# Mixed right sides moved behind the last low part, and a last step taken by halves of the tokens, in a two-layer fp32 kernel

## The chip, the cores and the metric

The kernel runs on one core of one Trainium2 chip. The metric is device time in microseconds (us) of one execution, the median of several. TensorE (PE in the rows) multiplies, VectorE (DVE), ScalarE (ACT) and GpSimd (POOL) work elementwise, and SyncE (SP) issues most of the DMAs. "Span" is the time from the first to the last instruction of the profiled execution.

## What is computed

Two transformer blocks, one after the other, on one sequence of 1024 tokens with 1024 features, all in fp32 accuracy:

```python
# first block
h = rmsnorm(x, norm1_g); proj = h @ w_in
... # differential attention (4 heads) and forgetting attention (8 heads)
x = x + mix @ w_out
h2 = rmsnorm(x, norm2_g)
x = x + (silu(h2 @ w_gate) * (h2 @ w_up)) @ w_down
x = rmsnorm(x, normf_g)
# second block
p = rmsnorm(x, g_attn) @ w_in_2
... # two causal convolutions and a stick-breaking attention (8 heads)
x = x + concat([y_a, y_b, y_c]) @ w_out_2
x = x + square(relu(rmsnorm(x, g_ffn) @ w_ff1)) @ w_ff2
out = rmsnorm(x, g_final)
```

## The kernel before

**Layout and precision.** Activations lie transposed: 128 features on the partitions, tokens along the row. A tensor of 1024 features is 8 tiles `e` of 128 x 1024, and a "half" is 512 tokens, the width of one PSUM bank. Every fp32 product is made of three fp32r matmuls: high part of the weights times high part of the right side (L1610), low weights times high right side (L1612), high weights times low right side (L1615). High parts of weights (`wh`) are made by ScalarE (L2176), low parts (`lows`, written over the loaded `values`) by GpSimd (L2414), for pieces of 128 x 512 that SyncE loads. The first matmul of a piece waits for its high part, the second for its low part; the third waits for the low part of the right side.

**The border between attention and feed-forward**, once per block (near 640 and near 1790 us). TensorE finishes the output projection: for each of 8 tiles `e`, six matmuls with the last row of the mix (`second_pass`). VectorE adds them to the residual (`second_evac`, L1974, two halves), ScalarE makes the high part of the scaled x (`post_hi`, L2327) and its square (`post_square`, L2337, into the single buffer P2), GpSimd adds the square to `mix` (L2473), and VectorE makes the low part (`post_lo`, L2030). Between the tiles, TensorE already runs the first two feed-forward tiles together, twelve matmuls for each row k of the right side (`dense_together`), two tiles behind. A sum over the partitions (L1655, the row sum) closes the norm; it waits for the seventh addition on GpSimd.

**Mixed right sides.** Later feed-forward tiles are multiplied in pairs by a scheme of seven products (`dense_seven`, P1 to P7) in place of eight. Four of the products need sums and differences of tiles of x: for each pair of tiles j four mixed right sides a. `right_sums` makes them: one ScalarE copy (`right_z`, L2186), four VectorE operations (`right_sum`, L2006, written to R0f), and for each a high part on ScalarE (L2191) and a low part on VectorE (L2013). They are first read by product P6 of the first pair, which stands after the first down step.

**Down steps.** `dense_down` multiplies hidden rows by the down weights, and `down_evac` adds each bank to x in place (L2017). The last one, `dense_last`, does tiles 0 and 1 together and then each tile 2 to 7 with both halves, 24 matmuls to a tile and one weight piece for both halves. Then comes the last norm: squares by whole tiles on ScalarE, added up on GpSimd, row sums into single columns (L1635), a root in a dozen small operations on (128, 4) (L1797 to L1818 and L2212), the factors spread over a bank by matmuls with the identity (L1646), a copy to `rstd` (L2240), 16 multiplications (11 on VectorE, L2146, straight from PSUM, 5 on GpSimd, L2468, of x scaled beforehand by ScalarE), and 16 stores of 256 KB.

**What sets the order.** `work_order` writes all steps down once, and a planner (`engine_orders`) lays each engine's part out by estimated costs and by what needs what. Each engine then runs its list strictly in order; a wait blocks all that stands behind it.

## Time and profile before

| quantity | value |
|---|---|
| runs, us | 2490.04 (median), 2487.53, 2492.13 |
| profiled execution, us | 2491.58 |
| its span, us | 2489.8 |
| TensorE busy, us of the span | 2439.9 (98%) |
| VectorE, ScalarE, GpSimd busy, us | 1716.4, 1019.4, 1045.0 |
| granted TensorE clock, mean share of full | 0.992 |

The profiled execution is 1.5 us above the median of the three runs. The view of 40 slices puts TensorE at nine tenths or more in nearly each slice. The waits of an engine are listed by its line and by the line that ended them; the timelines give start and duration of each instruction or merged group, and in square brackets the idle time before it.

### The profile page before, as it was taken

The numbers are of one execution on the slowest core, as the hardware profiler recorded it, in microseconds if no ns is written. First come the engines' busy times: TensorE is split into PE (matmuls) and PEld (weight loads), VectorE is DVE, ScalarE is ACT, GpSimd is POOL, SyncE is SP. The second block draws the span as 40 slices with busy tenths as digits, with TensorE's granted clock in tenths as the row PEclk, the third lists the DMA queues.
The fourth block names the chain that finished last, engine by engine and source line by source line (L and its number), as shares of the span: only waits on it lengthen the run. The fifth ranks groups of instructions, "written<-read, shape, count | busy, mean of one in ns | idle before, by whom it ended". The sixth has DMA issues, their size and how long they took to land.

```text
span 2489.8 us, 31274 instructions
## 1 busy us (share of the span) xinstructions
PE 2439.9 (98%) x11654; PEld 2002.7 (80%) x11654; DVE 1716.4 (69%) x2373; ACT 1019.4 (41%) x1727; POOL 1045.0 (42%) x718
## 2 busy tenths in 40 slices
PE   9999999999899999999999999999989999999998
PEld 7777788878688888888887878887868888888886
DVE  6777757673886666666679866776496676666663
ACT  6454555552533222222245435554252232323232
POOL 4666542211534444444454543431343343434344
PEclk9999999999999999999999999999999999999998
DMA  4211221132111111111123842223211111212121
GB/s 163 75 56 55 78 60 47 55 115 73 47 43 55 54 54 51 51 51 56 55 55 119 190 116 68 60 78 103 66 39 56 47 56 47 58 45 60 43 64 72
DMA packets 156261, 170.20 MB, mean 68 GB/s; under 512 B 11088, under 2 KB 114256, under 8 KB 155984
## 3 DMA queue, kind: packets, MB, share of 16 engines
q1 hardware_dynamic: 152944, 156.67, 21.0%
q0 software_dynamic: 3168, 11.54, 2.5%
q8 instruction: 94, 1.54, 0.3%
q14 instruction: 55, 0.45, 0.1%
HBM read 122.55 MB, written 15.20 MB: 55 GB/s over the span
## 4 chain that ended last, share of the span: by engine, by line
PE 87%; DVE 6%; ACT 2%; POOL 2%; issue 2%; DMA 1%; SPq 0%; DVEq 0%; ACTq 0%; POOLq 0%
PE PS L1610 24%; PE PS L1615 24%; PE PS L1612 24%; PE PS L1706 3%; PE PS L1693 2%; PE PS L1727 2%; PE PS L1724 2%; PE PS L1687 2%; DVE R0f L2006 1%; PE PS L1690 1%; DVE R L2030 1%; DVE X L1974 1%; PE PS L1692 0%; DVE Pb L1905 0%; DVE Pb L1903 0%
## 5 line engine op out<-in xcount | busy, mean ns | idle before, releaser
L1610 PE MATMUL PS<-R,wh 128*128 128x512 f32 x2952 | 1167.4, 395 | 5.3 <-DVE XP L1968 0.9
L1615 PE MATMUL PS<-R,wh 128*128 128x512 f32 x2952 | 1155.2, 391 | 13.0 <-DVE R L2030 12.6
L2414 POOL TENSOR_TENSOR lows<-values,wh 128x512 fp32r<-128x512 f32 (+1 forms) x410 | 594.2, 1451 | 1036.4 <-ACT wh L2176 928.2
L1612 PE MATMUL PS<-R,lows 128*128 128x512 f32 x2512 | 981.9, 391 | 1.4 <-POOL lows L2414 1.4
L1615 PEld LDWEIGHTS PS<-R,wh 128*128 128x128 f32 x2952 | 555.5, 188 | 137.5 <-DVE R L2030 17.8
L1610 PEld LDWEIGHTS PS<-R,wh 128*128 128x128 f32 x2952 | 556.4, 188 | 117.7 <-issue 3.6
L2176 ACT ACTIVATE wh<-values 128x512 fp32r<-128x512 f32 (+1 forms) x411 | 256.1, 623 | 726.2 <-PE PS L1615 693.4
L1612 PEld LDWEIGHTS PS<-R,lows 128*128 128x128 f32 x2512 | 473.3, 188 | 94.0 <-issue 3.6
L2017 DVE TENSOR_TENSOR X<-PS,X 128x512 f32<-128x512 f32 x400 | 272.2, 690 | 239.5 <-PE PS L1615 239.4
L2414 POOL TENSOR_TENSOR late_r<-late,wh 128x512 fp32r<-128x512 f32 x83 | 121.6, 1466 | 139.1 <-ACT wh L2176 100.1
L1612 PE MATMUL PS<-R,late_r 128*128 128x512 f32 x440 | 171.2, 389 | 0.0
L1994 DVE TENSOR_TENSOR stage<-PS,stage 128x512 f32<-128x512 f32 x154 | 104.6, 687 | 80.2 <-PE PS L1615 79.3
L2288 ACT ACTIVATE PT<-PS 128x512 fp32r<-128x512 f32 (+1 forms) x200 | 108.5, 553 | 92.2 <-PE PS L1706 85.3
L1693 PE MATMUL PS<-R 128*128 128x512 f32 (+2 forms) x288 | 117.1, 407 | 0.0
L1687 PE MATMUL PS<-R 128*128 128x512 f32 (+2 forms) x288 | 108.5, 377 | 8.5 <-ACT P L2271 3.7
L1891 DVE TENSOR_REDUCE sm<-PS 128x1 f32<-128x128 f32 (+7 forms) x128 | 95.3, 751 | 24.9 <-PE PS L1693 24.1
L1706 PE MATMUL PS<-ident,Pb 128*128 128x128 f32 x720 | 107.5, 274 | 4.3 <-DVE Pb L1903 2.8
L1915 DVE TENSOR_TENSOR_SCAN Pb<-TABF,vec 128x128 f32<-128x128 f32 (+3 forms) x64 | 95.6, 1499 | 20.6 <-ACT TABF L2280 11.1
L2176 ACT ACTIVATE wh<-late 128x512 fp32r<-128x512 f32 x83 | 52.3, 631 | 130.0 <-PE PS L1615 108.4
L1706 PEld LDWEIGHTS PS<-ident,Pb 128*128 128x128 f32 x720 | 86.2, 141 | 23.2 <-issue 8.0
L2271 ACT ACTIVATE Pb<-PS,sm 128x128 f32<-128x128 f32 (+3 forms) x96 | 71.1, 741 | 62.9 <-DVE sm L1891 61.7
L1612 PEld LDWEIGHTS PS<-R,late_r 128*128 128x128 f32 x440 | 82.6, 188 | 17.1
(269 smaller groups left out, 2811.9 us busy)
## 6 DMA issues: line engine op xcount, KB each, us to landing
values<-w_in_dram SPq DMA_DIRECT2D x88, 256.0 KB, 2.9
values<-w_ff_dram SPq DMA_DIRECT2D x88, 256.0 KB, 2.9
R<-R SPq DMA_DIRECT2D x96, 128.0 KB, 2.3
X<-X POOLq DMA_DIRECT2D x22, 512.0 KB, 5.8
values<-w_up_dram SPq DMA_DIRECT2D x38, 256.0 KB, 3.0
values<-w_gate_dram SPq DMA_DIRECT2D x36, 256.0 KB, 3.0
late<-w_ff_dram SPq DMA_DIRECT2D x36, 256.0 KB, 2.9
values<-w_down_dram SPq DMA_DIRECT2D x32, 256.0 KB, 2.7
```

Of the source, the lines that this page charges most:

```text
L1610: e.matmul(PS[:, b, :], wh, high, start=s["start"], stop=False)
L1612: e.matmul(PS[:, b, :], wl, high, start=False, stop=False)
L1615: m = e.matmul(PS[:, b, :], wh, low, start=False, stop=s["stop"])
L1687: e.matmul(S2[:, k0:k1], q, u.KH[:, a, k0:k1], start=True, stop=False)
L1693: m = e.matmul(S2[:, k0:k1], q, u.KL[:, a, k0:k1], start=False, stop=True)
L1706: m = e.transpose(PS[:, s["tb"], at:at + 128], T.Pb[:, s["slot"], par, 128 * kt:128 * kt + 128], T.ident[:, :])
L1915: e.tensor_tensor_scan(dst[:, ::-1], bt[:, ::-1], T.zeros(n), 1.0, ALU.mult, ALU.add).then_inc(*sg.up("p", j["key"]))
L1994: e.tensor_tensor(stage[s["i"]], PS[:, s["b"], :], stage[s["k"]], ALU.add).then_inc(*sg.up("seven", s["key"]))
L2017: e.tensor_tensor(x, PS[:, s["b"], :], x, ALU.add).then_inc(*sg.up("x", s["key"]))
L2176: e.activation(T.wh[:, piece.h, 0:m], T.wv[piece.v][:, 0:m], ACT.Copy).then_inc(*sg.up("w_hi", piece.n))
L2288: e.activation(T.PT[:, s["x"], 0, 0:m], PS[:, s["tb"], 0:m], ACT.Copy, bias=bias).then_inc(*sg.up("pt_hi", key))
L2414: e.tensor_tensor(T.wl[piece.v][:, 0:m], T.wv[piece.v][:, 0:m], T.wh[:, piece.h, 0:m].bitcast(F), ALU.subtract).then_inc(*sg.up("w_lo", pi ...
```

## The change

1. In `right_sums` the steps for pair j wait for the low part of the last tile (7) in place of the pair's own second tile. The planner then lists them behind the last `post_lo`.
2. `down_evac` of the first down step waits for the fourth mixed sum of its pair, which reads the x that it overwrites.
3. `dense_last` of the second block goes by halves from tile 2 on: all six tiles for half 0, then all six for half 1. The weight pieces of tiles 2 to 7 are loaded and split twice (six more pieces).
4. The squares of the last norm are made by halves (`end_half`), into stage buffers, and all added on VectorE (L1817 of the changed kernel) in place of GpSimd. The norm of half 0 is closed, its factors spread and its 8 tiles multiplied (all on VectorE) and stored while half 1 is multiplied. Of half 1, GpSimd multiplies three tiles, VectorE five. Six extra matmuls on ones stand between the sums and the spreading of half 1.
5. The dummy root that loaded ScalarE's table ahead is gone, and a few signals share semaphores.

```diff
@@ dense_last
+        if by_halves:
+            order += [(e, half, k) for half in range(2) for e in range(2, 8) for k in range(4)]
+        else:
+            order += [(e, half, k) for e in range(2, 8) for half in range(2) for k in range(4)]
...
-            piece = self.find("tile", name, e, t0)
+            piece = self.find("tile", name, e, t0, half if by_halves and e > 1 else 0)
...
@@ module level
-SCALED = [(0, 1), (0, 1, 2)]
+SCALED = [(), (0, 1, 2)]
@@ plan_ffn
+                for e in range(2, 8 if by_halves else 2):
                     O.plan_tile(down, e, 2 * i, 4)
@@ right_sums
-        x = [("post_hi", (tag, 2 * j + 1)), ("post_lo", (tag, 2 * j + 1))]
+        x = [("post_hi", (tag, 2 * j + 1)), ("post_lo", (tag, 7))]
@@ work_order
+    def end_half(e, half, done, first):
+        i, free = O.next_stage() if 0 < e < 7 + (half == 0) else (None, [])
+        O.step("end_square", e=e, half=half, done=list(done), first=list(first), i=i, free=free)
+        if i is not None:
+            O.stage_given[i] = [("accf", (e, half))]
+        if e in SCALED[half]:
+            O.step("scale", e=e, half=half)
+        if e < 7:
+            return
+        if half:
+            rows = [("mix", [[("accf", (6, 1))]] * 2), ("P2", [[("sqf", (7, 1))]] * 2)]
+        else:
+            rows = [("mix", [[("accf", (7, 0))]] * 2)]
+        beside = [] if half else [("dense", (O.last_dense[1][0], 3, 1))]
+        ready = O.rsqrt(rows, S, EPS2, "rstd", banks=[0, 1], halves=(half,), beside=beside)
+        if half:
+            O.step("busy", b=2, given=O.claim(2) + [("rs_sum", O.roots - 1)], n=6)
+        for e in SCALED[half]:
+            O.step("out_scaled", e=e, half=half, rs=ready[0])
+        for e in range(len(SCALED[half]), 8):
+            O.step("out", e=e, half=half, rs=ready[0], b=O.factor_banks[half])
@@ ffn, evac of a down step
-                O.step("down_evac", e=e, half=half, b=b, done=event, key=key)
+                O.step("down_evac", e=e, half=half, b=b, done=event, key=key, read=[("right_sum", (tag, e // 2, 3))] if i == 0 else [])
...
@@ vector_program
+        elif kind == "end_square" and s["i"] is not None:
+            k, half = s["e"], s["half"]
+            w.wait_ge(*sg.at("sqf", (0, half)))
+            w.wait_ge(*sg.at("sqf", (k, half)))
+            if k > 1:
+                w.wait_ge(*sg.at("accf", (k - 1, half)))
+            e.tensor_tensor(T.mix[:, cols(half)], T.mix[:, cols(half)], stage[s["i"]], ALU.add).then_inc(*sg.up("accf", (k, half)))
```

**Place 1: VectorE at the first border**, before, from the additions of tile 3 to the last low part. `X` from PSUM is the residual addition, `R1_50` the low part, `R0f_51` a mixed sum, `R0_49` the low part of a mixed right side.

```order
706 L1974 TENSOR_TENSOR X_52<-PS,XP1_79 128x512 x2
707 L2006 SCALAR_TENSOR_TENSOR R0f_51<-X_52,vec_71,R0f_51 128x512 x2
708 L2030 SCALAR_TENSOR_TENSOR R1_50<-X_52,vec_71,R1_50 128x1024
...
717 L2006 SCALAR_TENSOR_TENSOR R0f_51<-X_52,vec_71,R0f_51 128x512
718 L2030 SCALAR_TENSOR_TENSOR R1_50<-X_52,vec_71,R1_50 128x1024
719 L1974 TENSOR_TENSOR X_52<-PS,XP1_79 128x512 x2
720 L2006 SCALAR_TENSOR_TENSOR R0f_51<-X_52,vec_71,R0f_51 128x512 x2
721 L2030 SCALAR_TENSOR_TENSOR R1_50<-X_52,vec_71,R1_50 128x1024
722 L2013 TENSOR_TENSOR R0_49<-R0f_51,R0_49 128x512
```

The same place in the changed kernel, to the row sum's two evacuations (`stage_63<-PS`):

```order
710 L2000 TENSOR_TENSOR X_52<-PS,XP1_79 128x512 x2
711 L2058 SCALAR_TENSOR_TENSOR R1_50<-X_52,vec_71,R1_50 128x1024
712 L2000 TENSOR_TENSOR X_52<-PS,XP1_79 128x512
713 L2058 SCALAR_TENSOR_TENSOR R1_50<-X_52,vec_71,R1_50 128x1024
714 L2000 TENSOR_TENSOR X_52<-PS,XP1_79 128x512 x2
715 L2058 SCALAR_TENSOR_TENSOR R1_50<-X_52,vec_71,R1_50 128x1024
716 L2032 SCALAR_TENSOR_TENSOR R0f_51<-X_52,vec_71,R0f_51 128x512 x4
717 L1851 TENSOR_SCALAR stage_63<-PS 128x512 x2
```

Seven mixed sums stood between the low parts of x; now none does, and four stand directly behind the last one. The rest follow among the first tiles and the first down step.

**Place 2: TensorE at the end**, before:

```order
10518 L1615 MATMUL PS<-R_50,wh 128x512
10519 L1635 MATMUL PS<-ones,mix 128x1 x4
10520 L1635 MATMUL PS<-ones,P_61 128x1 x4
10521 L1635 MATMUL PS<-ones,mix 128x1 x4
10522 L1635 MATMUL PS<-ones,P_61 128x1 x4
10523 L1646 MATMUL PS<-identr,factors 128x128 x16
```

The changed kernel, the last matmuls of half 1 among them (lines 1627, 1629 and 1632 are the three products now):

```order
10462 L1654 MATMUL PS<-ones,mix 128x1 x4
...
10475 L1665 MATMUL PS<-identr,factors 128x128 x8
...
10521 L1654 MATMUL PS<-ones,mix 128x1 x4
10522 L1654 MATMUL PS<-ones,P_61 128x1 x4
10523 L1640 MATMUL PS<-ones 128x128 x6
10524 L1665 MATMUL PS<-identr,factors 128x128 x8
```

Four sums and eight spreading matmuls of half 0 have moved in among the matmuls of half 1; behind the last product eight sums, six extra ones and eight spreading matmuls are left.

**Place 3: VectorE at the end.** Before, 16 additions to x, two roots and 11 multiplications:

```order
1850 L2017 TENSOR_TENSOR X_52<-PS,X_52 128x512 x16
1851 L1797 TENSOR_SCALAR sm_72<-PS 128x4
...
1858 L1818 TENSOR_TENSOR factors_73<-sm_72,factors_73 128x4
1859 L1797 TENSOR_SCALAR sm_72<-PS 128x4
...
1866 L1818 TENSOR_TENSOR factors_73<-sm_72,factors_73 128x4
1867 L2146 SCALAR_TENSOR_TENSOR X_52<-X_52,vec_71,PS 128x512 x11
```

Changed, its last rows:

```order
1866 L2045 TENSOR_TENSOR X_52<-PS,X_52 128x512
1867 L2174 SCALAR_TENSOR_TENSOR X_52<-X_52,vec_71,PS 128x512 x2
1868 L1817 TENSOR_TENSOR mix_62<-mix_62,stage_63 128x512
1869 L2045 TENSOR_TENSOR X_52<-PS,X_52 128x512
1870 L1823 TENSOR_SCALAR sm_72<-PS 128x4
...
1877 L1844 TENSOR_TENSOR factors_73<-sm_72,factors_73 128x4
1878 L2174 SCALAR_TENSOR_TENSOR X_52<-X_52,vec_71,PS 128x512 x5
```

The additions of squares and the multiplications of half 0 now alternate with the additions to x; five multiplications remain behind the second root.

## Rows read from the trace of the kernel before

**Rows 1.** Waits of TensorE: engine, line, releaser: us in total, times, longest.

```profile
PE PS L1615 <- DVE R L2030: 12.6, 11, 2.5
PE PS L1687 <- ACT TABF L2280: 2.1, 1, 2.1
```

**Rows 2.** TensorE's timeline, first border: start, us, engine, line, operation, [idle before].

```profile
641.44 0.40 PE L1610 MATMUL PS<-R,wh 128*128 128x512 f32 x1
...
674.83 0.80 PE L1615 MATMUL PS<-R,wh 128*128 128x512 f32 x1 [2.52 <-DVE R L2030]
...
677.98 1.96 PE L1655 MATMUL PS<-mix,ones 128*128 128x512 f32 x4
...
680.01 0.40 PE L1612 MATMUL PS<-R,lows 128*128 128x512 f32 x1
```

**Rows 3.** VectorE at the first border: groups of 640 to 676 us, then its timeline.

```profile
L2006 DVE SCALAR_TENSOR_TENSOR R0f<-X,vec,R0f 128x512 f32<-128x512 f32 x7 | 16.0, 2303 | 0.0
...
666.79 2.30 DVE L2030 SCALAR_TENSOR_TENSOR R<-X,vec,R 128x1024 fp32r<-128x1024 f32 x1
669.01 1.27 DVE L1974 TENSOR_TENSOR X<-PS,XP 128x512 f32<-128x512 f32 x2
670.21 3.37 DVE L2006 SCALAR_TENSOR_TENSOR R0f<-X,vec,R0f 128x512 f32<-128x512 f32 x2
```

**Rows 4.** ScalarE's and GpSimd's timelines, first border.

```profile
651.88 1.15 ACT L2191 ACTIVATE R<-R0f 128x512 fp32r<-128x512 f32 x2 [2.84 <-DVE R0f L2006]
...
654.06 2.41 POOL L2473 TENSOR_TENSOR mix<-mix,P 128x1024 f32<-128x1024 f32 x1 [2.76 <-ACT P L2337]
...
673.58 3.42 POOL L2473 TENSOR_TENSOR mix<-mix,P 128x1024 f32<-128x1024 f32 x1 [0.55 <-ACT P L2337]
```

**Rows 5.** TensorE's timeline, second border.

```profile
1793.04 0.39 PE L1615 MATMUL PS<-R,wh 128*128 128x512 f32 x1
...
1828.92 1.98 PE L1655 MATMUL PS<-mix,ones 128*128 128x512 f32 x4 [0.36 <-POOL mix L2473]
...
1830.97 0.39 PE L1612 MATMUL PS<-R,lows 128*128 128x512 f32 x1
```

**Rows 6.** Busy time by stretch: us, PE, PEld, DVE, ACT, POOL, PEclk, DMA share, GB/s.

```profile
675.00:680.00 5.00, 5.00 (x12) 3.33 (x13) 5.00 (x6) 1.22 (x2) 1.99 (x1) 0.69 0.00 0
```

**Rows 7.** A mixed sum behind the first border, and where the second block's down step begins.

```profile
711.42 0.74 DVE L2006 SCALAR_TENSOR_TENSOR R0f<-X,vec,R0f 128x512 f32<-128x512 f32 x1
...
1859.36 2.47 DVE L2017 TENSOR_TENSOR X<-PS,X 128x512 f32<-128x512 f32 x4
...
1860.09 0.50 PE L1610 MATMUL PS<-R,wh 128*128 128x512 f32 x1 [0.61 <-DVE X L2017]
```

**Rows 8.** TensorE's timeline at the end, and one spreading group in mid-kernel.

```profile
2462.75 0.39 PE L1612 MATMUL PS<-R,lows 128*128 128x512 f32 x1
...
2469.78 0.40 PE L1615 MATMUL PS<-R,wh 128*128 128x512 f32 x1
...
2472.61 1.03 PE L1635 MATMUL PS<-ones,P 128*128 128x1 f32 x8
2473.64 3.73 PE L1646 MATMUL PS<-identr,factors 128*128 128x128 f32 x16
...
1495.46 1.00 PE L1646 MATMUL PS<-identr,factors 128*128 128x128 f32 x8
```

**Rows 9.** The other engines' timelines at the end.

```profile
2470.94 0.63 ACT L2340 ACTIVATE P<-X 128x512 f32<-128x512 f32 x1 [1.14 <-DVE X L2017]
...
2471.89 0.16 DVE L1797 TENSOR_SCALAR sm<-PS 128x4 f32<-128x4 f32 x1 [0.99 <-PE PS L1635]
...
2476.25 7.33 DVE L2146 SCALAR_TENSOR_TENSOR X<-X,vec,PS 128x512 f32<-128x512 f32 x11 [0.77 <-ACT rstd L2240]
2476.36 6.18 POOL L2468 TENSOR_TENSOR X<-X,rstd 128x512 f32<-128x512 f32 x5 [7.28 <-ACT rstd L2240]
...
2485.68 1.32 SPq L2583 DMA_DIRECT2D out_dram<-X  x2
```

More of the change, by code:

```diff
@@ L381, in plan_seven, with find @@
         return factors
-    def find(self, kind, name, e, k):
-        for piece in self.pieces:
-            if (piece.kind, piece.name, piece.e, piece.k) == (kind, name, e, k):
-                return piece
+    def find(self, kind, name, e, k, n=0):
+        found = [piece for piece in self.pieces if (piece.kind, piece.name, piece.e, piece.k) == (kind, name, e, k)]
+        return found[n]
     def take_place(self, base):
@@ L606, in dense_last @@
             self.mm(b, (src, *places[k][half]), piece, k, k == 0, k == 3, given, ready[k][half] if e < 2 else [],
-                    [key] if k == 3 else [], k == 3 and half == 1)
+                    [key] if k == 3 else [], frees)
             if k == 3:
@@ L614, in dense_last, with rsqrt @@
                         self.split_piece()
-    def rsqrt(self, rows, dim, eps, dst, banks=None, halves=(0, 1)):
+    def rsqrt(self, rows, dim, eps, dst, banks=None, halves=(0, 1), beside=()):
         if len(self.dense_banks) == 8:
@@ L635, in rsqrt @@
         for half, (b, given) in zip(halves, taken):
-            self.step("rs_cast", n=n, half=half, b=b, given=[("rs_mean", n)] if half == halves[0] else given)
+            self.step("rs_cast", n=n, half=half, b=b, given=list(beside) + ([("rs_mean", n)] if half == halves[0] else given))
             self.step("rs_out", n=n, half=half, b=b, dst=dst)
@@ L1006, in work_order, with plan_ffn @@
     need1, need2 = lambda p: 2 * p - 1, lambda p: p - 2
-    def plan_ffn(straight, pairs, downs, need, plain, down):
+    def plan_ffn(straight, pairs, downs, need, plain, down, by_halves=False):
         factors = []
@@ L1044, in work_order @@
     plan_start("w_out2", [("w_ff1", 0), ("w_ff1", 1)])
[L1045 removed]
+    factors2 = plan_ffn([("w_ff1", 2), ("w_ff1", 3)], [(("w_ff1", t), ("w_ff1", t + 1)) for t in range(4, 32, 2)], 16, need2, 1, "w_ff2", True)
     O.step("gains")
@@ L1072, in work_order @@
         O.split_piece()
-    O.step("busy", b=7)
+    O.step("busy", b=7, given=[], n=14)
     O.step("h_in", e=0, half=1)
@@ L1219, in post_x @@
         gain_free = [("accg_sum", (name, e - 2))] if e > 2 else []
-        for half in range(2) if e == 7 and name in ("nf", "fin") else [None]:
+        for half in range(2) if e == 7 and name == "nf" else [None]:
             mine = list(done) if half is None else [done[half]]
@@ L1273, in start_ffn @@
         O.lend_stages(MIDDLE, O.rstd_ready)
-    def make_rstd(dim, eps, name):
-        rows = [("mix", [[("acc2", (name, 6))] + O.rstd_ready] * 2), ("P2", [[("sq2", (name, 7, half))] for half in range(2)])]
-        O.rstd_ready = [event for half in range(2) for event in O.rsqrt(rows, dim, eps, "rstd", halves=(half,))]
+    def end_half(e, half, done, first):
[19 more added lines that the diff above has]
+            O.step("out", e=e, half=half, rs=ready[0], b=O.factor_banks[half])
     def hidden_free(tag, t):
@@ L1289, in hidden, with ffn @@
         return places[t % 2][half], [("dense", (tag, "down", t // 2 - 1) if t > 1 else "straight " + tag)]
-    def ffn(tag, straight, factors, downs, need, plain, down, evacs, hr, post):
+    def ffn(tag, straight, factors, downs, need, plain, down, evacs, hr, post, by_halves=False):
         O.dense_banks, O.dense_at = [2, 3, 0, 1], 0
@@ L1619, in tensor_program @@
             w.wait_ge(*sg.at("ones", 0))
-            for k in range(14):
-                e.matmul(PS[:, s["b"], 128:256], T.ones[:, :], T.ones[:, :], start=k == 0, stop=k == 13)
+            for event in s["given"]:
+                w.wait_ge(*sg.at(*event))
+            for k in range(s["n"]):
+                e.matmul(PS[:, s["b"], 128:256], T.ones[:, :], T.ones[:, :], start=k == 0, stop=k == s["n"] - 1)
         elif kind == "lambda":
@@ L2015, in vector_program @@
             x = T.XF[:, s["e"], cols(s["half"])]
+            for event in s["read"]:
+                w.wait_ge(*sg.at(*event))
             w.wait_ge(*sg.at(*s["done"]))
@@ L2340, in scalar_program @@
                 e.activation(square_row(T, name, k)[:, cc], x[:, cc], ACT.Square).then_inc(*sg.up("sq2", (name, k, s["half"])))
+        elif kind == "end_square":
+            k, cc = s["e"], cols(s["half"])
+            for event in s["done"] + s["first"] + s["free"]:
+                w.wait_ge(*sg.at(*event))
+            sq = T.mix[:, cc] if k == 0 else T.P2[:, cc] if s["i"] is None else stage[s["i"]]
+            e.activation(sq, T.XF[:, k, cc], ACT.Square).then_inc(*sg.up("sqf", (k, s["half"])))
         elif kind == "post_gain":
```

51 lines of the change are left out of this document (20 added, 31 removed).

## Prediction, written before the changed kernel was run

> **What bounds the kernel now.** I read four views in this order: the shares of busy time, the waits of TensorE, the timelines of the two borders, and the timeline of the end. TensorE is busy for 98% of the span, so only its pauses, its slow stretches and what stands behind its last matmul can be won. The list of its waits has one large entry: the third product (L1615) waits for the low part of x (L2030), 12.6 us in 11 pieces; all others are 2.1 us and less [rows 1]. These pauses stand at the two borders. Between 2462.75 and 2469.78 us 31 matmuls start, one each 0.227 us [rows 8]. By the written order 117 such matmuls stand between 641.44 us and the row sum, so undisturbed it would start at 641.44 + 26.5 = 668.0; it starts at 677.98 [rows 2]. Ten us are lost there, some 7 in pauses (the last one 2.52), the rest because matmuls went at half speed: the granted clock is 0.69 from 675 to 680 [rows 6], so at 1.2 GHz for part of it and at 2.4 for the rest, after TensorE had paused four times since 657 us.
>
> Why the low parts are late is in VectorE's rows. It never rests there, and seven mixed sums take 16.0 us, 2.30 each [rows 3], where one that meets nothing takes 0.74 [rows 7]. So the sums are long because of what runs beside them, and the low parts and the residual additions queue behind them: tile 7's additions begin only at 669.01, its low part after 673.5 [rows 3]. ScalarE's list suffers as well: it stood 2.84 us at a high part of a mixed side, with the next square behind it, and GpSimd's addition idled 2.76 us for that square [rows 4].
>
> The Trainium skill ("SBUF — State Buffer", section "SBUF: two separate sides") says that VectorE, with two SBUF inputs, and GpSimd share a port pair as an exclusive lock, so the loser blocks for the whole instruction. By that rule a moved sum costs 0.74 where GpSimd rests and up to 3 where it works; without it, 2.3 wherever it stands, which is the slower rival below. The two prices of the sum above speak for the lock.
>
> **Part 1, the borders.** The seven sums go behind the last low part. What is late next? Not the low part: TensorE needs per tile 18 matmuls, 4.1 us; VectorE then has two additions (1.27 the pair [rows 3]) and one low part of the same length. It is GpSimd's chain: a square can't be made before the last one is added (one buffer), so a tile costs addition 2.41 [rows 4] + square 1.05 = 3.5, and where a weight split and a low part of x fall between, 2.41 + 1.1 + 1.2 = 4.7. I walk it with these: the third addition starts when its square needn't wait behind the mixed high part, at 651.8 in place of 654.06 [rows 4]; one interval of 3.5 and three of 4.7 follow, so the seventh starts at 669.4. It takes 2.4 plus 0.2 to 0.6 that a mixed sum holds it: end 672.1, where it was 673.58 + 3.42 = 677.0 [rows 4]. The row sum starts at 672.3, and 2.0 us later (677.98 to 680.01 [rows 2]) come plain matmuls at 674.3. The planner has put six matmuls more ahead of the row sum, so the counterpart of this point before is 680.01 + 4 x 0.227 = 680.9. Gain 6.6. On the way TensorE waits about 1.8 us for the last low part (ready 668.2, wanted 666.4) and 1.2 for the row sum; I take no fall of the clock from two waits so short, where before it fell after more than 6 us of them.
>
> The second border is the same pattern 1151.6 us later (1793.04 against 641.44), but its plain matmuls began 0.6 us sooner in the pattern (1830.97 - 1151.6 = 679.4) [rows 5]. Gain 6.0.
>
> Bounds: above, if TensorE never waits, 680.0 - 670.0 = 10.0 and 9.4. Below, if GpSimd's chain stays as it is, the row sum starts at 677.05, plain matmuls 2.0 later, against 680.9: 1.8; at the second, where it already was the releaser (0.36) [rows 5], 1.0. I take the walk, which stands between, because the two long idle times of the chain have named causes that go.
>
> **Given back behind the border.** The work isn't gone: 32 mixed operations per border still stand on VectorE ahead of the first use, and the additions to x of the first down step now wait for them. At the second border VectorE was already the late one there: its four additions begin at 1859.36 without a rest ahead, and TensorE waits 0.61 for them [rows 7]. Up to those additions the changed list has one or two operations fewer than before, but TensorE arrives 1.4 us sooner in relation to the row sum (six matmuls done ahead), so the wait grows by about half a us. At the first border the backlog between the first additions and product P6 grows from 3 to 12 mixed operations of 0.74, 6.7 us, in a stretch of 21.8 us of TensorE where VectorE has 9.8 of additions; I put its cost at 1.5 us (0 to 4). Together -2. Borders net: 6.6 + 6.0 - 2 = **10.6**.
>
> **Part 2, the end.** Before, 20.0 us lie between the start of the last product (2469.78) and the end of the span (2489.8) [rows 8]. Now, counted from the start of the last product: the addition to x ends at 1.1, the square at 1.8 (2470.94 + 0.63 [rows 9]); the last four sums take 1.0 (2472.61 [rows 8]; those over `mix` go ahead) to 2.8; from sums to factors 1.8 (2471.89 to 2473.64 [rows 8, 9]): 4.6. The eight spreading matmuls take 1.0 at the full clock (the row at 1495.46 has the same eight [rows 8]) or 3.73 / 2 = 1.9 at the half clock that these rows had. The six extra matmuls fill TensorE's wait; whether they hold the clock no row tells. Copy and hand-over 0.6: 6.2 to 7.1. Five multiplications on VectorE, 7.33 / 11 = 0.67 each, end at 9.6 to 10.4; three on GpSimd, 6.18 / 5 = 1.24 each [rows 9], at 9.9 to 10.8. The last store is issued by then + 0.65, and lands 2.8 later (2485.68 + 1.32 to 2489.8 [rows 9]): 13.4 to 14.3. The eight stores of half 0 are long out.
>
> Against it stand the sums and the spreading of half 0 in the middle of half 1, where nothing hides them on TensorE: 0.9 + 1.0 = 1.9. VectorE needs 2.1 us from sums to factors and TensorE has 12 matmuls, 2.7 us, between: no wait. Gain 20.0 - 1.9 - 13.9 = **4.2**, range 1 to 6 (a wait at half 0's factors, or both halves at the better clock).
>
> **Edits costed at nothing.** Six more loads, ScalarE copies and GpSimd splits: a piece now lasts 12 matmuls, 2.7 us, and a split 1.3, while GpSimd loses seven additions of 2.4; if a split came late, TensorE would wait up to 1.3 for each of six. VectorE gains 13 additions of 0.7 in a stretch where it rested three quarters. By the same rule of the skill as above each may block a split for its length; the splits are two pieces ahead. The table load for the root (1.3) moves into a wait for squares. SyncE's loads stand ahead of all stores in both lists. The planner also shifts single blocks at about ten places of the second attention; the longest wait there is 2.1 [rows 1], so I put it at 0, with 2 either way.
>
> **Sum.** 10.6 + 4.2 = 14.8 below the profiled execution's 2491.58 (1.8 of it lies outside the span and stays), 2476.8. The median of the runs is 1.5 below that execution: **2475**.
>
> **Rivals.**
> 1. TensorE becomes the only bound at the borders: 10.0 + 9.4, nothing given back, 4.2 at the end: 23.6, 2466.5. For it: VectorE's and ScalarE's work per tile is well below 4.1 us. Against: GpSimd's chain of 3.5 to 4.7 a tile. Chance 0.12.
> 2. GpSimd's chain takes the place of the low part and is as late as before: 2.8 at the borders, 4.2 at the end: 7.0, 2483. For it: at the second border it was the releaser already. Chance 0.14.
> 3. The borders' gain comes back in full as waits at the first down step and at P6, or the new order of the end costs what it saves; one of the two alone is left, at most 4: 2486 to 2491, no change that can be told. Chance 0.09.
> 4. Slower. The moved work is as dear behind the border as inside it: seven sums at 2.3 and eight low parts with 1.6 more each are 28.9 us a border. VectorE starts on them 6.6 sooner and has about 6 idle in the first down step, so TensorE would wait 16 there: each border 9.4 worse, both 19, less 4.2: about 2505. It decides from 1.4 us more per moved operation on. Against: the row of 0.74 [rows 7] is from just that stretch. Chance 0.05.
>
> **How the numbers follow.** Forecast 0.60 (own range 2470 to 2480). A measurement tells about 0.2%, 5 us, from no change. Faster by more: forecast and rivals 1 and 2, 0.86; within: 0.09; slower: 0.05. The range 2467 to 2483 takes in the ceiling and the floor of the borders and leaves out rivals 3 and 4 and half of the tails of 1 and 2.
>
> **What would show it.** Right: TensorE's waits for the low part fall from 12.6 to under 4 us and it waits 1 to 2 us for GpSimd's addition at each row sum; the clock stays full at 675 us; mixed sums average near 1 us; about 13.5 to 14.5 us from the last product to the end; stores of half 0 under way ahead of it. Wrong: waits for the additions to x of several us behind the borders (rival 4 or 3), a GpSimd addition still ending near 677 (rival 2), no wait at the row sums (rival 1), or the second spreading at the half clock together with a wait at the first.

## Result and profile after

The changed kernel takes 2474.49 us (median of 4 runs, 2473.24 to 2478.29) against 2489.54 us for the kernel before, run beside it: ratio 0.9942, 95% interval 0.9924 to 0.9959, so 15.0 us faster. The prediction said 2475, by 14.8 us. The sum is met, but its terms are not: the borders gave more than forecast, the end less, and a term put at zero was not zero.

The profiled execution took 2473.24 us (span 2471.5), 18.3 less than that of before. Of this 2.7 us can't come from the change: a wait that both kernels have far ahead of the first border, in lists that do not differ up to there, ends at 587.32 us before and at 584.62 after. It is chance between two executions: 1.8 us of it arise between 515 and 553 us, where the granted clock of before is 0.50 from 535 to 538 us and that of the changed kernel 1.00 from 532 to 536. The kernel below that has the border of before (the end alone) also ends its last wait for a low part at 672.33, where before ends it at 674.83 [rows 2]. So at the first border the changed kernel's times plus 2.7 are compared with those of before.

TensorE's waits, changed kernel (engine, line, releaser: us in total, times, longest):

```profile
PE PS L1632 <- DVE R L2058: 3.2, 4, 1.4
...
PE PS L1665 <- DVE factors L1842: 1.6, 1, 1.6
...
PE PS L1674 <- POOL mix L2504: 1.4, 2, 0.7
PE PS L1627 <- DVE X L2045: 1.3, 1, 1.3
```

The waits for the low part are 3.2 us where they were 12.6 [rows 1], and GpSimd's addition ends a wait at each row sum. Both were forecast. The wait for `factors` was not.

**First border**, changed kernel: TensorE's timeline (start, us, engine, line, operation, [idle before]), GpSimd's, VectorE's, VectorE's groups of 640 to 676 us, and the stretch of 675 to 680 us (busy times, then the granted clock, 1.00).

```profile
665.38 0.50 PE L1632 MATMUL PS<-R,wh 128*128 128x512 f32 x1 [1.42 <-DVE R L2058]
669.33 1.98 PE L1674 MATMUL PS<-mix,ones 128*128 128x512 f32 x4 [0.69 <-POOL mix L2504]
...
671.38 0.40 PE L1629 MATMUL PS<-R,lows 128*128 128x512 f32 x1
```

```profile
666.44 2.84 POOL L2504 TENSOR_TENSOR mix<-mix,P 128x1024 f32<-128x1024 f32 x1
```

```profile
666.24 6.13 DVE L2032 SCALAR_TENSOR_TENSOR R0f<-X,vec,R0f 128x512 f32<-128x512 f32 x4 [0.92 <-ACT R0f L2214]
...
674.08 0.74 DVE L2032 SCALAR_TENSOR_TENSOR R0f<-X,vec,R0f 128x512 f32<-128x512 f32 x1
```

```profile
L2058 DVE SCALAR_TENSOR_TENSOR R<-X,vec,R 128x1024 fp32r<-128x1024 f32 x7 | 15.0, 2150 | 5.3 <-ACT R L2352 5.3
L2032 DVE SCALAR_TENSOR_TENSOR R0f<-X,vec,R0f 128x512 f32<-128x512 f32 x6 | 7.5, 1259 | 1.1 <-ACT R0f L2214 0.9
```

```profile
675.00:680.00 5.00, 5.00 (x23) 4.14 (x23) 3.54 (x6) 4.54 (x7) 0.00 (x0) 1.00 0.00 0
```

GpSimd's seventh addition starts at 666.44 + 2.7 = 669.1 (forecast 669.4) and ends at 672.0 (672.1); the row sum starts at 672.0 (672.3), plain matmuls at 674.1 (674.3). The clock that stood at 0.69 [rows 6] stays full. VectorE now rests 5.3 us in this stretch, where it rested 0.3; its low parts still take 2.15 us beside GpSimd. From the wait of 0.17 that both kernels have (it ends at 640.39 before, at 637.69 here) to the row sum, 121 matmuls start before and 127 here, so the counterpart of 674.1 stands six matmuls of 0.227 behind 680.01, at 681.4. The prediction counted four, and so wrote 680.9. 7.3 us are gained; its own walk to 674.3 would have given 7.1 with six, where it says 6.6. The four mixed sums behind the last low part take 1.53 each while GpSimd still works, the next 0.74.

**Second border and its down step**, TensorE:

```profile
1806.35 0.50 PE L1632 MATMUL PS<-R,wh 128*128 128x512 f32 x1 [1.41 <-DVE R L2058]
...
1810.29 1.98 PE L1674 MATMUL PS<-mix,ones 128*128 128x512 f32 x4 [0.70 <-POOL mix L2504]
...
1840.75 0.50 PE L1627 MATMUL PS<-R,wh 128*128 128x512 f32 x1 [1.26 <-DVE X L2045]
```

The same pattern as at the first, and the wait for the additions to x is 1.26, where it was 0.61 [rows 7]: 0.65 us given back, half a us was forecast.

**Half 0 in the last step**: TensorE, ScalarE, VectorE and GpSimd, then the stretch of 2445 to 2449 us, where the granted clock is 0.58 on average, so at 1.2 GHz for most of it.

```profile
2437.79 0.95 PE L1654 MATMUL PS<-ones,mix 128*128 128x1 f32 x8
...
2443.14 1.10 PE L1665 MATMUL PS<-identr,factors 128*128 128x128 f32 x8 [1.56 <-DVE factors L1842]
...
2445.55 0.63 PE L1632 MATMUL PS<-R,wh 128*128 128x512 f32 x1
```

```profile
2438.69 0.72 ACT L2255 ACTIVATE X<-X,vec 128x512 f32<-128x512 f32 x1
2439.43 1.28 ACT L2240 ACT_TABLE_LOAD   x1
2440.73 0.21 ACT L2240 ACTIVATE sm<-sm 128x4 f32<-128x4 f32 x1
```

```profile
2441.77 1.23 DVE L1842 CAST factors<-sm 128x4 fp32r<-128x4 f32 x1
```

```profile
2441.71 1.26 POOL L2445 TENSOR_TENSOR lows<-values,wh 128x512 fp32r<-128x512 f32 x1 [2.36 <-ACT wh L2204]
```

```profile
2445.00:2449.00 4.00, 4.00 (x12) 3.09 (x12) 3.01 (x6) 0.64 (x1) 0.00 (x0) 0.58 0.35 131
```

The mean of half 0 is there at 2438.94, the factors only at 2443.19. In between ScalarE scales a tile of half 1 (0.72), loads the table (1.28) and takes the root, and a copy of four columns lasts 1.23 us: it starts 0.06 us after a weight split on GpSimd does and ends 0.03 us after it. TensorE waits 1.56, and then eight matmuls stand 0.43 us apart instead of 0.227: 1.6 us more. In all, 18.2 us lie between the last product ahead of half 0's sums (2437.56) and the last product of all (2455.77). The 57 products in between need 12.9, so 5.3 us went to half 0's sums and spreading, for which the prediction had 1.9.

**Behind the last product** (start 2455.77): TensorE and SyncE's last store. The profile has two rows for each matmul of the sums and of the extra ones: x8 are four sums, x12 the six extra ones.

```profile
2455.77 0.39 PE L1632 MATMUL PS<-R,wh 128*128 128x512 f32 x1
2456.14 1.05 PE L1654 MATMUL PS<-ones,mix 128*128 128x1 f32 x8
2457.61 1.05 PE L1654 MATMUL PS<-ones,P 128*128 128x1 f32 x8 [0.41 <-ACT P L2371]
2458.72 2.93 PE L1640 MATMUL PS<-ones 128*128 128x128 f32 x12
2461.30 1.44 PE L1665 MATMUL PS<-identr,factors 128*128 128x128 f32 x8
```

```profile
2468.00 0.64 SPq L2618 DMA_DIRECT2D out_dram<-X  x1
```

From the last product to the end 15.7 us pass, where 20.0 did [rows 8, 9] and 13.4 to 14.3 were forecast. The factors were ready at 2460.49, but the six extra matmuls, at half clock (the granted clock is 0.58 from 2458 to 2462), held TensorE until 2461.3. By this one profile the end cost 1.0 us instead of saving 4.2: 20.0 - 5.3 - 15.7.

### The profile page after: what moved, and what is told of

The parts are those of the page before. It is cut to its first block, busy times and chain, and to the rows that moved or that the text cites. A ratio compares the mean times of both kernels' runs of the same rounds, so it can differ in the third digit from the quotient of the medians.

```text
span 2471.5 us, 31314 instructions
## 1 busy us (share of the span) xinstructions
PE 2431.6 (98%) x11658; PEld 1998.3 (81%) x11658; DVE 1720.1 (70%) x2387; ACT 1022.8 (41%) x1737; POOL 1038.4 (42%) x716
## 4 chain that ended last, share of the span: by engine, by line
PE 85%; DVE 4%; POOL 4%; ACT 2%; issue 2%; DMA 2%; SPq 0%; POOLq 0%; DVEq 0%; ACTq 0%
PE PS L1627 24%; PE PS L1632 24%; PE PS L1629 24%; PE PS L1725 3%; PE PS L1712 2%; PE PS L1746 2%; PE PS L1743 2%; PE PS L1706 2%; DMA X<-X 1%; POOL mix L2504 1%; PE PS L1709 1%; POOL lows L2445 1%; DVE Pb L1931 0%; POOL stage L2456 0%; DVE R0f L2032 0%
## 5 line engine op out<-in xcount | busy, mean ns | idle before, releaser
L2445 POOL TENSOR_TENSOR lows<-values,wh 128x512 fp32r<-128x512 f32 (+1 forms) x416 | 607.2, 1462 | 1035.4 <-ACT wh L2204 924.4
L2445 POOL TENSOR_TENSOR late_r<-late,wh 128x512 fp32r<-128x512 f32 x83 | 122.9, 1480 | 136.8 <-ACT wh L2204 95.4
```

Source lines behind the costliest of these rows:

```text
L2445: e.tensor_tensor(T.wl[piece.v][:, 0:m], T.wv[piece.v][:, 0:m], T.wh[:, piece.h, 0:m].bitcast(F), ALU.subtract).then_inc(*sg.up("w_lo", pi ...
```

## Experiments

The runs of before beside these had medians of 2489.5 (first four kernels), 2489.7 (next four) and 2488.4 us (last three), so kernels of different groups are compared by what each lies below its own runs of before.

| kernel | median, us | range | against before |
|---|---|---|---|
| borders alone | 2473.18 | 2472.32 to 2477.94 | 0.9940 (0.9927 to 0.9952) |
| end alone | 2488.86 | 2485.51 to 2489.64 | 0.9994 (0.9985 to 1.0003) |
| before, additions cut (sums of squares left out) | 2469.38 | 2467.22 to 2471.64 | 0.9921 (0.9908 to 0.9935) |
| changed, dummy root | 2470.73 | 2469.50 to 2472.27 | 0.9927 (0.9913 to 0.9941) |
| borders alone, no moved blocks | 2475.80 | 2473.68 to 2477.30 | 0.9950 (0.9937 to 0.9962) |
| end alone, dummy root | 2485.38 | 2483.66 to 2487.13 | 0.9986 (0.9976 to 0.9995) |
| dummy root, no extra matmuls | 2471.65 | 2470.48 to 2473.14 | 0.9933 (0.9920 to 0.9947) |
| dummy root, additions on VectorE | 2468.63 | 2466.51 to 2471.64 | 0.9922 (0.9909 to 0.9934) |
| changed, spreading later | 2473.56 | 2472.46 to 2473.91 | 0.9939 (0.9925 to 0.9952) |
| dummy root, last three on VectorE | 2472.04 | 2470.64 to 2472.58 | 0.9933 (0.9920 to 0.9945) |
| dummy root, last five on VectorE | 2472.72 | 2467.27 to 2476.10 | 0.9935 (0.9921 to 0.9948) |

### The two parts apart

Borders alone: the kernel before with

```diff
-        x = [("post_hi", (tag, 2 * j + 1)), ("post_lo", (tag, 2 * j + 1))]
+        x = [("post_hi", (tag, 2 * j + 1)), ("post_lo", (tag, 7))]
...
+            for event in s["read"]:
+                w.wait_ge(*sg.at(*event))
```

> The kernel before with part 1 alone (mixed right sides wait for the low part of tile 7, the first down step waits for the mixed sum that reads its x); the end is that of before. Its list of work is that of the changed kernel up to the last step, the moved blocks of the second attention with it. Theory A, from the trace of the changed kernel: nearly all of the gain comes from here (6.8 us first border, some 4 in the second attention, 6 second border, 0.6 given back), so 14 to 16 us below the kernel before, about 2474 to 2475. Theory B, the sum of the prediction: 10.6 us, about 2479. Both: TensorE's waits for the low part near 3 us, one wait of 0.7 to 1.4 for GpSimd's addition at each row sum, no fall of the clock at the borders.

End alone: the changed kernel with the first of these undone and no `read`.

> The changed kernel with part 1 undone: mixed right sides wait for their own pair again and stand between the low parts; the last step goes by halves. Theory A: the end gains nothing or 1 us, because the wait of 1.6 at the factors of half 0, some 1.7 of slow clock behind it and 1.8 for its sums and spreading stand against 4.3 won behind the last product: 2488 to 2490. Theory B, the prediction: 4.2 less than before, about 2485.5. Either way the waits for the low part are back at 12 to 13 us.

Measured: 16.3 and 0.65 us. Theory A held for both: the borders' part is worth as much as the whole change or more, and the end, for which I had 4.2, next to nothing. One of its reasons was absent from the profile of the end alone: it has the same wait of 1.56 us at the factors of half 0 (the spreading starts at 2460.46), but no slow matmul behind it; the granted clock is 1.00 from 2460 to 2466. There 3.7 us went to half 0's sums and spreading, and 20.0 - 3.7 - 15.7 = 0.6 is what the medians say. The two kernels' traces can be laid beside each other at waits that both have. End alone, TensorE:

```profile
741.55 0.50 PE L1627 MATMUL PS<-R,wh 128*128 128x512 f32 x1 [0.78 <-DVE stage L2020]
...
1467.79 0.41 PE L1693 MATMUL PS<-ident,stage 128*128 128x128 f32 x2 [0.96 <-DVE stage L1951]
...
1683.32 0.47 PE L1627 MATMUL PS<-R,wh 128*128 128x512 f32 x1 [0.62 <-ACT R L2343]
1687.95 0.50 PE L1706 MATMUL PS<-R 128*128 128x512 f32 x1 [2.10 <-ACT TABF L2305]
```

Borders alone, the same places:

```profile
735.07 0.50 PE L1610 MATMUL PS<-R,wh 128*128 128x512 f32 x1 [0.85 <-DVE stage L1994]
...
1461.29 0.41 PE L1674 MATMUL PS<-ident,stage 128*128 128x128 f32 x2 [0.96 <-DVE stage L1925]
...
1676.95 0.64 PE L1687 MATMUL PS<-R 128*128 128x512 f32 x1 [2.03 <-ACT TABF L2282]
```

The distances are 6.5, 6.5 and 11.0 us; the first border began 0.5 later in the borders alone (a wait of 0.17 ends at 638.38 against 637.91), so it gave 7.0 net, where 5.1 was forecast (6.6 less 1.5): of the 7.2 to 7.3 gained at the row sum 0.3 was given back. Between 1468 and 1688 us 4.5 more are gained, for which I had 0, and a wait of 0.62 is gone there. Behind the second border's down step the distance is 16.7: 5.8 net, where 5.5 was forecast.

### The moved blocks of the second attention

Borders alone, with each engine's list of the second attention taken from the kernel before:

```diff
-    orders = engine_orders(T, sg, work_order(T))
+    orders = spliced(T, sg, sem)
...
+        orders[engine] = [steps[n] for n in b[:first] + a[first:last] + b[last:]]
```

(`a` is the plan without part 1, `b` the one with it; `first` and `last` are the borders of the second attention.)

> The kernel before with part 1 alone, as in the run of the borders alone, but in the second attention every engine's list is that of the kernel before: none of the single blocks that the planner shifts there is moved. Theory A: about 4.4 of the 16.3 us came from these shifts (between the wait at 1467 us and the one at 1688 us of the kernel with the end alone, the one with the borders alone needs 4.4 us less), so this kernel is near 2477.5 and the borders themselves gave 12. Theory B, the prediction's 0 with 2 either way: the shifts are worth nothing on their own and the difference in the traces is chance from one execution to the next; 2473 to 2474.

Measured 2475.80: 2.6 us more than with the moved blocks, between the two theories, and the ranges of the runs overlap. Its timeline shows where the blocks matter:

```profile
1677.05 0.47 PE L1613 MATMUL PS<-R,wh 128*128 128x512 f32 x1 [0.51 <-ACT R L2323]
...
1680.39 0.50 PE L1690 MATMUL PS<-R 128*128 128x512 f32 x1 [2.10 <-ACT TABF L2285]
```

The wait for ScalarE at 1677 us is back. Against end alone this kernel is 5.3 us ahead at the wait of 1468 us (it starts at 1462.50 here) and 7.6 at that of 1688: 2.3 of the 4.5 us came without any moved block. Some 1.6 of these 2.3 are the clock: the granted clock of the end alone is 0.77 from 1480 to 1495 us, and that of the borders alone and of this kernel 0.89 from 1475 to 1490. The first moved block of the borders alone stands only near 1540 us, so this is chance between executions. About 2.2 us (2.6 by the medians) are left for the blocks, by one profile of each kernel. The borders without them give 13.9 us by the medians and 12.8 by the two stretches of the traces above.

### Why a mixed sum was dear inside the border

In the kernel before, the order kept, GpSimd's additions at both borders take 8 columns:

```diff
-            e.tensor_tensor(T.mix[:, :], T.mix[:, :], square_row(T, name, k), ALU.add).then_inc(*sg.up("acc2", (name, k)))
+            c = slice(0, 8) if name in ("n2", "n3") and not isinstance(e, Uncounted) else slice(0, S)
+            e.tensor_tensor(T.mix[:, c], T.mix[:, c], square_row(T, name, k)[:, c], ALU.add).then_inc(*sg.up("acc2", (name, k)))
```

(`Uncounted` is the planner's stand-in for an engine: the planner still sees 1024 columns, so the order stays.)

> The kernel before with its order unchanged, but at the two borders GpSimd's additions of the squares take 8 columns in place of 1024, so the sums of squares are left out there for the other tokens. It asks why seven mixed sums took 2.30 us each inside the border. Theory A (they block on GpSimd, which shares something with VectorE): with GpSimd nearly idle they fall to 0.7 to 1.0 each, low parts and additions to x come in time, the waits for the low part fall from 12.6 to under 3 us, and the kernel is 15 to 19 us faster, about 2472, with the mixed sums still in their old place. Theory B (they are dear through what ScalarE and TensorE do beside them, or because of where they stand): they stay near 2.3 and the kernel gains less than 4 us.

Groups of VectorE and GpSimd, 640 to 672 us (count, then busy us and mean ns), and that stretch's busy time on TensorE (the first number behind 32.00) and granted clock (the 1.00):

```profile
L2030 DVE SCALAR_TENSOR_TENSOR R<-X,vec,R 128x1024 fp32r<-128x1024 f32 x6 | 7.8, 1296 | 1.9 <-ACT R L2327 1.9
L2006 DVE SCALAR_TENSOR_TENSOR R0f<-X,vec,R0f 128x512 f32<-128x512 f32 x11 | 9.5, 873 | 0.0
```

```profile
L2474 POOL TENSOR_TENSOR mix<-mix,P 128x8 f32<-128x8 f32 x7 | 4.1, 590 | 9.5 <-ACT P L2337 9.5
```

```profile
640.00:672.00 32.00, 31.94 (x137) 25.42 (x137) 27.46 (x33) 24.75 (x34) 12.37 (x13) 1.00 0.19 58
```

Theory A, and more than it asked for: 20.1 us. With the sums in their old place a mixed sum takes 0.87 instead of 2.30 [rows 3], and TensorE is busy for 31.94 of 32 us, where before it was for 27.43. A low part takes 1.30 on average; before, in the same window, it took 1.67, most of them 1.27 and two of the seven 3.04 and 2.30. So it was the mixed sums above all that were dear, and neither the place nor ScalarE nor TensorE made them so; GpSimd's additions did. The 20.1 us are not the mixed sums' alone: the same cut also shortens GpSimd's chain of additions, for which the squares and the row sum wait. The Trainium skill ("SBUF — State Buffer", section "SBUF: two separate sides") calls this an exclusive lock that VectorE takes with two SBUF inputs; the trace agrees, also in that the additions to x, which read PSUM, take 0.68 us in the changed kernel's border beside GpSimd's work.

### The table load in front of half 0's root

The changed kernel with one more root on ScalarE, whose result nobody reads; it only has the table loaded earlier:

```diff
             e.activation(sq, T.XF[:, k, cc], ACT.Square).then_inc(*sg.up("sqf", (k, s["half"])))
+            if (k, s["half"]) == (6, 0) and not isinstance(e, Uncounted):
+                e.activation(T.sm[:, 112:113], T.ones[:, 0:1], ACT.Sqrt)
```

> The changed kernel with a dummy root on ScalarE behind the square of tile 6, half 0, so that the table load (1.28 us) no longer stands between the sums of half 0 and its root; all else stands in the same order. Theory A: the load was the largest part of the wait at the factors, so the wait falls from 1.56 to 0.3 to 0.6 us, the clock doesn't fall behind it, and the kernel gains 2.5 to 3 us, about 2471.5. Theory B: the small cast of the factors meets GpSimd's split again (1.23 us where others of its size take 0.16), wherever it then lands, and still sets the end of the chain; the wait goes only to 1.0 to 1.5 and the clock still falls, gain under 1 us.

ScalarE, VectorE and TensorE of this kernel:

```profile
2434.20 1.28 ACT L2373 ACT_TABLE_LOAD   x1
```

```profile
2441.58 0.17 DVE L1842 CAST factors<-sm 128x4 fp32r<-128x4 f32 x1
```

```profile
2442.38 1.00 PE L1665 MATMUL PS<-identr,factors 128*128 128x128 f32 x8
...
2456.20 1.60 PE L1640 MATMUL PS<-ones 128*128 128x128 f32 x12
2457.93 1.10 PE L1665 MATMUL PS<-identr,factors 128*128 128x128 f32 x8
```

3.8 us faster than the changed kernel by the medians, a us more than expected; the two 95% intervals against before overlap, so the traces must say where it comes from. The load is hidden, half 0's factors are ready 2.2 us behind its sums (4.4 in the changed kernel, 2.1 forecast), the copy starts before the next split and takes 0.17, TensorE doesn't wait, no matmul is slow behind the spreading, and the six extra ones run at full speed: from the last product (2453.25) to the end (2467.7) 14.5 us. Against the changed kernel 3.5 us are gone ahead of the last product and 1.3 behind it; the execution stood 1.0 later ahead of the sums.

With the end alone:

> The changed kernel with part 1 undone and the dummy root behind the square of tile 6, half 0: the end alone, without the table load between sums and factors of half 0. Theory A: the load was the one error in the prediction's 4.2 us for the end, so 3.5 to 4.5 us below the kernel before, about 2485.3. Theory B: the gain of the dummy root depends on the borders' part or on the position of GpSimd's split, and the end gives under 2.5 us, above 2487.

Measured 2485.38: 4.3 us below the kernel before, and 14.5 us from the last product (2467.87) to the end (2482.4). That is the prediction's 4.2, though the interval allows 1.2 to 6.0. By the traces it is 20.0 - 1.8 - 14.5 = 3.7, with 1.8 for half 0's sums and spreading, where 1.9 was forecast. So the load, the copy that it pushed onto a split, and the wait and slow matmuls that came with them were nearly the whole error of part 2.

A second way to take the wait away leaves load and copy where they are and puts the spreading twelve matmuls later:

```diff
-        beside = [] if half else [("dense", (O.last_dense[1][0], 3, 1))]
+        beside = [] if half else [("dense", (O.last_dense[1][0], 4, 1))]
```

> The changed kernel with one number changed: the spreading of half 0 stands twelve matmuls (one tile of half 1) later on TensorE, behind tile 4 in place of tile 3. The table load and the small cast that meets GpSimd's split stay where they are. Theory A: the wait of 1.56 at the factors, and the 1.7 us of half clock behind it, come from nothing but factors 1.6 us too late for a place 12 matmuls (2.7 us) behind the sums; with 5.4 us there is no wait and no fall, and the kernel gains the same 3 to 3.8 us as with the dummy root, about 2471. Theory B: what lowered the clock was the group of small sums and spreading matmuls, or the load, not the wait; then the wait goes but matmuls at half speed stay, and the gain is 1.5 us, about 2473.

```profile
2444.75 1.00 PE L1665 MATMUL PS<-identr,factors 128*128 128x128 f32 x8
...
2454.22 1.05 PE L1654 MATMUL PS<-ones,mix 128*128 128x1 f32 x8 [0.94 <-DVE mix L1817]
...
2457.41 2.93 PE L1640 MATMUL PS<-ones 128*128 128x128 f32 x12
2459.99 1.95 PE L1665 MATMUL PS<-identr,factors 128*128 128x128 f32 x8
```

In the middle it went as Theory A says: no wait, and no slow matmul behind it, with load and slow copy (1.26 us) as before. That the wait was what lowered the clock is not shown by it, since the end alone had the wait and no fall. And the gain over the changed kernel was 0.9 us by the medians and none against the runs of before beside each (14.8 and 15.0), not 3 to 3.8: half 0's multiplications, begun later, now stand between VectorE's last additions, the sums of half 1 wait 0.94 for one of them, and nearly all behind them ran at half speed. Neither theory had that.

### The six extra matmuls

With the dummy root, the six left out (`n = 0` at that step, its waits kept):

> The changed kernel with the dummy root and without the six extra matmuls on ones between the last sums and the spreading of half 1. With them the spreading of eight took 1.10 us. Theory A: the extra matmuls keep the clock up; without them TensorE rests 1.8 us and the eight take 1.6 to 1.9 us, the copy and the five multiplications follow as much later, and the kernel is 0.5 to 0.8 us slower than with them, about 2471.4. Theory B: a rest of 1.8 us does not lower the clock by itself; the spreading starts at the same moment and takes 1.0 to 1.1 us, no difference.

```profile
2460.76 1.10 PE L1666 MATMUL PS<-identr,factors 128*128 128x128 f32 x8 [1.79 <-DVE factors L1843]
```

TensorE rests 1.79 us and the eight then take the same 1.10; 14.5 us from the last product (2456.09) to the end (2470.6), as with them. So Theory B: here they neither change the clock of the spreading nor cost anything. The 0.9 us between the medians lie within the runs' spread and not in this stretch.

### What is late next at the borders

The seven additions of squares on VectorE, with the dummy root (the step's code moves from GpSimd's program to VectorE's):

> The changed kernel with the dummy root, and the seven additions of squares of each border on VectorE in place of GpSimd (128x1024, two SBUF inputs, one stream more on VectorE, none on GpSimd but the weight splits). Theory A: what is left late at the borders is GpSimd's chain and the low parts that wait for it (low parts 2.1 to 2.7 us beside an addition or a split, 1.3 without); per tile VectorE then has 1.3 for the two additions to x, 1.3 for the low part, 1.3 for the square and 4.1 to do it in, so the waits of 1.42 and 0.70 at each border go and the kernel gains 3 to 4 us, about 2467. Theory B: VectorE becomes the late engine (a split of 1.3 us may block each of its three), the last low part comes as late or later, and the kernel gains nothing or loses up to 5 us.

```profile
665.13 1.98 PE L1674 MATMUL PS<-mix,ones 128*128 128x512 f32 x4
...
706.24 0.50 PE L1627 MATMUL PS<-R,wh 128*128 128x512 f32 x1 [1.70 <-DVE X L2050]
```

```profile
657.20 1.29 DVE L2063 SCALAR_TENSOR_TENSOR R<-X,vec,R 128x1024 fp32r<-128x1024 f32 x1 [0.15 <-ACT R L2357]
```

Low parts are back at 1.3 us, no wait for them nor at the row sums is left at the borders; but at the first down step TensorE now waits 1.70 for the additions to x. 2.1 us faster than the dummy root alone by the medians, a little over half of what Theory A gave, and with overlapping intervals. The wait is of the kind of the forecast's give-back of 1.5, but VectorE also has seven additions more here, so it does not show what a faster border alone would give back. At 2468.63 us, 0.9922 of before, it has the lowest median of the kernels that compute everything.

Fewer additions moved, to relieve VectorE (the last three; the last five):

> The changed kernel with the dummy root, and at each border the last three additions of squares (tiles 5, 6, 7) on VectorE, the first four on GpSimd as in the changed kernel. With all seven on VectorE the waits for the low part and at the row sum were gone, but the first down step waited 1.70 us for its additions to x, which it had not before. Theory A: the end of GpSimd's chain alone set the two waits, so they go here too, and VectorE, with four additions fewer, is less behind at the first down step (0 to 1 us there): 1 us better than with all seven, about 2467.5. Theory B: the wait at the down step depends on the mixed sums standing behind the last low part, not on the additions; same as with all seven, 2468 to 2469, or GpSimd's first four still delay the low parts.

> As the kernel before it, with the additions of tiles 3 to 7 on VectorE and those of 1 and 2 on GpSimd. Theory A: between the two neighbours, 2467.5 to 2468.5, with no wait for low parts and some 1 us at the first down step. Theory B: the place of the change-over does not matter at all, within 0.5 us of both.

The last three on VectorE, TensorE's timeline:

```profile
666.15 1.98 PE L1678 MATMUL PS<-mix,ones 128*128 128x512 f32 x4 [1.02 <-DVE mix L1819]
...
734.62 0.80 PE L1631 MATMUL PS<-R,wh 128*128 128x512 f32 x1 [2.32 <-DVE stage L2029]
```

Both miss. With three, the waits for the low part go and that at the first down step too, but the row sum waits 1.02 for VectorE's last addition, and the wait at 734 us, 0.85 in the changed kernel, is 2.32. Its profiled execution also stood at half speed where that of the dummy root did not: the granted clock is 0.66 from 734 to 739 us, and its tail took 15.7 us from the last product. The medians, 2472.0 and 2472.7, are 16.4 and 15.7 us below the runs of before beside them, where the dummy root is 18.8: no gain over it. With five, the waits are nearly those of all seven (1.67 at the down step, and 0.42 at the row sum), its profiled span is 2467.3, but its runs spread over 9 us, so its median doesn't rank it.

## Why the prediction was right, and where it was not

- **What bounds, and why the sums were dear: right, and shown.** The cut additions alone bring the first border to full use of TensorE. The split of the ten us lost there was wrong: "some 7 in pauses", the rest by half speed. From 674.83 to 677.98 us seven matmuls start 0.45 us apart, and that is 1.6 us; the other 8.4 lie in and around the pauses.
- **The walk of GpSimd's chain: right within 0.3 us** at each of its points up to the plain matmuls, as was "no fall of the clock from two waits so short". What it was compared with was wrong: six matmuls moved ahead of the row sum are 1.4 us and not "4 x 0.227". With that, its own walk gives 7.1 us and 7.3 are measured. Its assumption that a low part takes 1.3 us was wrong too (2.15, it meets GpSimd's work); the wait for the last one, 1.42, still lies inside the 1.8 allowed, and the row sum behind it waits for GpSimd. Mixed sums average 1.26 in the border's stretch, where I had written near 1.
- **Given back: half right.** The second border's wait grew by 0.65 (0.5 forecast). Of the first's 1.5 only 0.3 to 0.4 appeared.
- **The attention's moved blocks, "0, with 2 either way": too low.** They bring 2.2 to 2.6 us, at the edge of that range; one wait for ScalarE went.
- **Part 2, 4.2: wrong; 0.7 by the medians of the end alone, -1.0 by the changed kernel's profile.** The step that failed: "VectorE needs 2.1 us from sums to factors and TensorE has 12 matmuls, 2.7 us, between: no wait", together with "the table load for the root (1.3) moves into a wait for squares". With the dummy root of the kernel before gone, nothing but half 0's root itself asks for the table, so the load stands behind the mean and not in any rest of ScalarE; and the 2.1 us took the small operations at their best. From sums to factors it was 4.4, and TensorE waited 1.56. With the slow end, and in the changed kernel's profile (not in that of the end alone) slow matmuls behind the wait, this cost 3.8 us by the medians. Take the load away and the term is about right (4.3 by the medians, 3.7 by the traces).
- **The sum, 14.8, came out (15.0) because errors cancel, and that is luck:** borders 10.6 forecast against 13.9 (12.8 by the traces), moved blocks 0 against 2.6, end 4.2 against 0.7. The terms measured apart add up to 17.0, 1.9 more than the change; that is within the spread of runs that differ by 3 to 6 us among themselves, and the slow matmuls that only the changed kernel's profile has in its last step are 1.6 of it, if its other runs have them too. The two profiled executions, 18.3 us apart, split as 2.7 ahead of the first border, 6.9 by it, 3.8 in the second attention (1.7 of them the clock near 1490 us), 5.9 by the second border, and 1.0 lost at the end.
- **Rivals.** None of the four happened. Part of the third did (the end costs what it saves), and the text named its sign: the second spreading slowed together with a wait at the first.

## What to carry to other kernels

When an engine's instructions are several times longer in one stretch than in another, ask which neighbour's work runs beside them, and cut that work in a trial with the order kept: one such run tells the cause from its rivals, and about how much there is to gain. When a chain of tiny operations is moved out of the tail into the stream, add up everything that its engines do in between, a table load and the bad moment of each tiny operation among it, and leave room for the worst. A term of zero for "blocks that the planner moves elsewhere" is a guess; it deserves a range of its own. And a forecast sum that comes out says little of its terms: here running each part alone showed two of them off by some 3 us, in opposite directions.

## What the runs showed of the hardware that was not expected

- A VectorE copy of 128x4 (0.16 to 0.17 us) lasts 1.23 when it starts 0.06 us after a GpSimd split of 1.26, and again 1.23 in the end alone and 1.26 with the spreading later, each time just behind the start of a split. The small operations ahead of it in the chain began before the split. The Trainium skill ("SBUF — State Buffer", section "SBUF: two separate sides") extends the lock to copies in a two-port mode; the trace agrees, as far as this copy runs in such a mode, which no run here shows.
- GpSimd's addition of 8 columns still takes 0.59 us, against 2.4 for 1024.
- Slow matmuls: in the changed kernel's profile the granted clock averaged 0.58 over the 4 us from 2445 on, behind the pause of 1.56 at half 0's factors; in that of the end alone, with the same pause at the same place, it was 1.00. After 1.42 and 0.69 at each border it was not lowered, and the spreading behind a pause of 1.79 at the very end still took 1.10. The tail ran at half speed in the changed kernel and the end alone, with the spreading later (after pauses of 0.94 and 0.21) and with the last three additions on VectorE (extra matmuls 2.60, spreading 1.82), and its matmuls at full speed in the other five kernels with the dummy root (1.10 for the spreading). The length of the pause ahead does not sort these, and what does stays open. A difference of one or two us between two single profiles can be this alone: from 1480 to 1495 us the granted clock was 0.77 in the profile of the end alone and 0.89 in that of the end alone with the dummy root, which has the same lists there, and that was 1.6 us.
